# Scores of the diagonal and of neighbours by element products, the mask added in PSUM, and the last two output tiles finished in SBUF

## The reference

```python
u = rmsnorm(x, g_mix); proj = u @ w_in          # columns: q k v | hg_q hg_f hg_i hg_og | gate_a gate_b
# A: stick-breaking attention, 8 heads of 128, strictly causal
z = q @ k.T * scale
log_keep = where(s < t, log_sigmoid(-z), 0); later = reverse_cumsum(log_keep) - log_keep
w = exp(where(s < t, log_sigmoid(z) + later, -inf)); y_a = w @ v
# B: HGRN2 recurrence, 8 heads, state 128 x 128:  S_t = diag(f_t) S_{t-1} + (1-f_t)^T v_t,  o_t = q_t S_t
y_b = rmsnorm(o) * silu(hg_og)
m = sigmoid(gate_a) * (y_a @ p_a) + sigmoid(gate_b) * (y_b @ p_b)
h = x + m @ w_o
up = causal_depthwise_conv(rmsnorm(h) @ w_up, width 3); gate, val = split(up)
out = h + (silu(gate) * val) @ w_down            # d_ff = 5632
```

## Time and profile before

| | us |
|---|---|
| median of 3 runs | 2868.12 (2868.11 to 2868.18) |
| profiled execution | 2867.83 |
| its span | 2866.3 |
| PE busy | 2844.1 (99%) |
| DVE busy | 1852.0 (65%) |
| ACT busy | 1175.4 (41%) |
| POOL busy | 283.5 (10%) |

### The profile page before, as it was taken

One profiled execution on the slowest core, in us unless ns is written; L12 is line 12 of the kernel. 1 busy time (PEld: TensorE's weight loads), 2 busy tenths in 40 slices (PEclk: granted clock), 3 DMA queues, 4 the chain that ended last, 5 costly groups with the idle time before them and its releaser, 6 DMA issues.

```text
span 2866.3 us, 46361 instructions
## 1 busy us (share of the span) xinstructions
PE 2844.1 (99%) x16324; PEld 2504.7 (87%) x16324; DVE 1852.0 (65%) x3256; ACT 1175.4 (41%) x1575; POOL 283.5 (10%) x384
## 2 busy tenths in 40 slices
PE   8999999999999999999999999999999999999998
PEld 6888888888888888888889999999999999999997
DVE  6545454545454546444458988878878887887883
ACT  5333323232323233333345544444444444454443
POOL 1000101020201000000000111101111111110112
PEclk9999999999999999999999999999999999999999
DMA  4242425252423332444445655556555565555657
GB/s 159 79 138 84 146 84 148 92 149 89 114 93 96 97 92 96 155 146 139 139 160 156 141 137 139 134 137 137 137 137 133 137 140 131 140 135 135 139 136 144
DMA packets 157157, 366.96 MB, mean 128 GB/s; under 512 B 18192, under 2 KB 27536, under 8 KB 156560
## 3 DMA queue, kind: packets, MB, share of 16 engines
q1 hardware_dynamic: 111888, 273.41, 30.4%
q0 software_dynamic: 45056, 90.72, 17.4%
HBM read 303.24 MB, written 78.12 MB: 133 GB/s over the span
## 4 chain that ended last, share of the span: by engine, by line
PE 97%; DMA 1%; issue 1%; DVE 0%; POOL 0%; ACT 0%; SPq 0%; POOLq 0%; ACTq 0%; DVEq 0%
PE bank L1440 15%; PE bank L1442 15%; PE bank L1441 15%; PE bank L1604 10%; PE bank L1606 10%; PE bank L1605 10%; PE bank L1622 5%; PE bank L1621 5%; PE bank L1623 5%; PE bank L1486 2%; PE bank L1473 1%; PE bank L1531 1%; PE bank L1517 1%; DMA w_raw<-wstream 0%; POOL out_t L509 0%
## 5 line engine op out<-in xcount | busy, mean ns | idle before, releaser
L1604 PE MATMUL bank<-v_hi,w_hi 128*128 128x256 f32 x2464 | 698.0, 283 | 2.1 <-issue 1.5
L1606 PE MATMUL bank<-v_hi,w_lo 128*128 128x256 f32 x2464 | 697.3, 283 | 0.0
L1605 PE MATMUL bank<-v_lo,w_hi 128*128 128x256 f32 x2464 | 697.3, 283 | 0.0
L720 ACT ACTIVATE w_hi<-w_raw 128x896 fp32r<-128x896 f32 (+1 forms) x528 | 444.8, 846 | 555.2 <-DVE w_raw L1245 390.7
L1440 PE MATMUL bank<-u_hi,w_hi 128*128 128x512 f32 x1408 | 555.2, 394 | 11.0 <-DVE u_lo L894 10.3
L1252 DVE TENSOR_TENSOR w_lo<-w_raw,w_hi 128x896 fp32r<-128x896 f32 (+1 forms) x528 | 499.5, 952 | 102.1 <-ACT w_hi L720 101.0
L1442 PE MATMUL bank<-u_hi,w_lo 128*128 128x512 f32 x1408 | 549.5, 390 | 0.0
L1441 PE MATMUL bank<-u_lo,w_hi 128*128 128x512 f32 x1408 | 549.0, 390 | 0.0
L868 DVE TENSOR_TENSOR w_lo<-w_raw,w_hi 128x1024 fp32r<-128x1024 f32 x240 | 292.7, 1222 | 341.0 <-ACT w_hi L527 338.8
L1604 PEld LDWEIGHTS bank<-v_hi,w_hi 128*128 128x128 f32 x2464 | 472.8, 192 | 5.5 <-issue 3.8
L1605 PEld LDWEIGHTS bank<-v_lo,w_hi 128*128 128x128 f32 x2464 | 472.9, 192 | 1.8 <-issue 0.2
(11 more groups left out here) (210 smaller groups left out, 3303.8 us busy)
## 6 DMA issues: line engine op xcount, KB each, us to landing
w_raw<-wslots SPq DMA_DIRECT2D x504, 256.0 KB, 2.7
w_raw<-wstream SPq DMA_DIRECT2D x240, 512.0 KB, 3.5
out_t<-stage POOLq DMA_DIRECT2D x168, 256.0 KB, 4.3
sums_scratch<-wfirst POOLq DMA_DIRECT2D x24, 448.0 KB, 11.6
w_raw<-sums_scratch SPq DMA_DIRECT2D x24, 448.0 KB, 3.3
gates_scratch<-g_out POOLq DMA_DIRECT2D x32, 256.0 KB, 2.6
g_in<-gates_scratch POOLq DMA_DIRECT2D x16, 512.0 KB, 4.0
x_in<-x_t SPq DMA_DIRECT2D x8, 512.0 KB, 9.9
```

The source lines that it names most:

```text
L720: act.activation(w4_hi[ring][:, 0:width], w4_raw[ring][:, 0:width], ACT.Copy).then_inc(w4_hi_ready, 1)
L1604: nc.tensor.matmul(out, wh, xh, start=kp == 0 and half == 0, stop=False, skip_group_check=True)
L1605: nc.tensor.matmul(out, wh, xl_, start=False, stop=False, skip_group_check=True)
L1606: ins = nc.tensor.matmul(out, wl, xh, start=False, stop=kp == KP - 1, skip_group_check=True)
```

## The change

1. The mask matmuls are gone. PE's z_done comes after the four score matmuls, DVE adds the mask (now fp32 in SBUF) to the four diagonal blocks in PSUM, and ACT waits for z_masked.
2. The diagonal scores and the level-0 scores (each token with its left neighbour in a pair) are sums over channels of element products. DVE multiplies them into prod (512 + 256 columns), ACT copies prod to prod_hi (fp32r), DVE subtracts to prod_lo, and PE sums over partitions with a matmul of ones against prod_hi and prod_lo. Level 0 is left out of `levels`, and DVE's copy of k into xl at level 0 is gone.
3. The last two down tiles are not copied by ACT and not added by POOL. SP loads the present sums of output tiles 14 and 15 into SBUF, DVE adds the PSUM banks, and SP stores plainly. Tile 15 is computed in two halves of 256 columns in banks 0 and 1 (in_halves: for each half, three matmuls of 256 columns per f, and half_done after the first half of the last slot).

```diff
@@ SP, after the weight loads
+            sp_.wait_ge(slot_done, SLOTS - RING)
+            sp_.dma_start(part_sum[:, :], out_t[:, c * SEQ:]).then_inc(part_sum_in, 16)
+            sp_.wait_ge(last_ready, 1)
+            sp_.dma_start(out_t[:, c * SEQ:(c + 1) * SEQ], last_out[:, 0:SEQ]).then_inc(last_stored, 16)
+            for half in range(2):
+                at_ = SEQ + HALF * half
+                sp_.wait_ge(last_ready, 2 + half)
+                sp_.dma_start(out_t[:, c * SEQ + at_:c * SEQ + at_ + HALF],
+                              last_out[:, at_:at_ + HALF]).then_inc(last_stored, 16)
+            sp_.wait_ge(last_stored, 16 * 3)
@@ POOL
-            for d, c in DOWNS:
+            for d, c in DOWNS[:-LAST]:
@@ ACT
-                            act.wait_ge(z_done, per(1, 1))
+                            act.wait_ge(z_masked, per(1, 1))
...
                             act.wait_ge(vt_done, per(2, 2))
                             act.activation(v_tok[:, :], misc_b[:, :], ACT.Copy).then_inc(vt_ready, 1)
+                            act.wait_ge(prod_ready, per(2, 2))
+                            act.activation(prod_hi[:, :], prod[:, :], ACT.Copy).then_inc(prod_hi_ready, 1)
@@ DVE, level(0)
-                    steps.did(dve.tensor_copy(X[:, :, 0, :], K[:, :, 0, :]))
...
+                if L == 0:
+                    pairs = prod[:, SEQ:NP].rearrange("p (g r) -> p g r", r=1)
+                    dve.tensor_tensor(pairs, X[:, :, 1, :], K[:, :, 0, :], ALU.mult).then_inc(prod_ready, 1)
@@ DVE, p == 6 + 3 * late
+                            dve.wait_ge(z_done, per(1, 1))
+                            for b in range(NB):
+                                ins = dve.tensor_tensor(Z[b][:, b * P:(b + 1) * P], Z[b][:, b * P:(b + 1) * P],
+                                                        mask[:, :], ALU.add)
+                            ins.then_inc(z_masked, 1)
@@ DVE, p == 11 + late and p == 12 + late
                             take(5, v_in[:, :])
+                            dve.tensor_tensor(prod[:, 0:SEQ], qn[:, :], kn[:, :], ALU.mult).then_inc(prod_ready, 1)
                             level(0)
                             level(1)
...
+                            dve.wait_ge(prod_hi_ready, per(1, 1))
+                            dve.tensor_tensor(prod_lo[:, :], prod[:, :], prod_hi[:, :].bitcast(F32),
+                                              ALU.subtract).then_inc(prod_lo_ready, 1)
                             level(2)
                             level(3)
@@ DVE, at the end
+            dve.wait_ge(part_sum_in, 16)
+            dve.wait_ge(slot_done, SLOTS - 1)
+            dve.tensor_tensor(last_out[:, 0:SEQ], bank[GROUP + DOWNS[-2][0] % GROUP][:, :], part_sum[:, 0:SEQ],
+                              ALU.add).then_inc(last_ready, 1)
+            for half in range(2):
+                at_ = HALF * half
+                if half == 0:
+                    dve.wait_ge(half_done, 1)
+                else:
+                    dve.wait_ge(slot_done, SLOTS)
+                dve.tensor_tensor(last_out[:, SEQ + at_:SEQ + at_ + HALF],
+                                  bank[half][:, 0:HALF],
+                                  part_sum[:, SEQ + at_:SEQ + at_ + HALF], ALU.add).then_inc(last_ready, 1)
@@ PE, after unit 6
-                                nc.tensor.matmul(Z[b][:, b * P:SEQ], kn[:, b * P:(b + 1) * P], qn[:, b * P:SEQ],
-                                                 start=True, stop=False, skip_group_check=True)
-                                ins = nc.tensor.matmul(Z[b][:, b * P:(b + 1) * P], ident_r[:, :], nmask_r[:, :],
-                                                       start=False, stop=True, skip_group_check=True)
+                                ins = nc.tensor.matmul(Z[b][:, b * P:SEQ], kn[:, b * P:(b + 1) * P], qn[:, b * P:SEQ],
+                                                       start=True, stop=True, skip_group_check=True)
@@ PE, after unit 13
-                            for b in range(NB):
-                                nc.tensor.matmul(Z[2][:, b * P:(b + 1) * P], kn[:, b * P:(b + 1) * P],
-                                                 qn[:, b * P:(b + 1) * P], start=True, stop=True)
+                            pe.wait_ge(prod_lo_ready, per(1, 1))
+                            for part in (prod_hi, prod_lo):
+                                nc.tensor.matmul(Z[2][:, :], ones_r[:, :], part[:, 0:SEQ],
+                                                 start=part is prod_hi, stop=part is prod_lo)
+                            for part in (prod_hi, prod_lo):
+                                nc.tensor.matmul(Z[0][:, 0:NP - SEQ], ones_r[:, :], part[:, SEQ:NP],
+                                                 start=part is prod_hi, stop=part is prod_lo)
@@ PE, last tile
+                    if d == DOWNS[-1][0]:
+                        ins = in_halves(ring, kk, fs, first)
+                        continue
```

More of the change, by code:

```diff
@@ L65 @@
 STAGES, END_STAGES, END = 2, 8, 168
+LAST = 2
 def feed_forward_slots():
@@ L126 @@
 EXP_LN_SET, SIGMOID_SET = 6, 2
-DVE_STEPS1, ACT_STEPS1 = 110, 18
+DVE_STEPS1, ACT_STEPS1 = 108, 18
 class Steps:
@@ L179, in build_program @@
     at = R3 + 12 * NZ
+    NP = SEQ + SEQ // 2
+    prod, prod_lo = sb("prod", NP, 32 * 1024), sb("prod_lo", NP, 32 * 1024, F32R)
+    prod_hi = sb("prod_hi", NP, 32 * 1024 + 4 * NP, F32R)
     S = sb("S", NB * SEQ, at)
@@ L202, in build_program @@
     ident_r = sb("ident_r", P, c0 + 12 * P, F32R)
-    nmask_r = sb("nmask_r", P, c0 + 16 * P, F32R)
+    mask = sb("mask", P, c0 + 16 * P)
     ones_r = sb("ones_r", P, c0 + 20 * P, F32R)
@@ L231, in build_program @@
     stage_end = [sb(f"stage_end{j}", SEQ, R2 + T * j) for j in range(END_STAGES)]
+    part_sum = sb("part_sum", LAST * SEQ, R2 + T * END_STAGES)
+    last_out = sb("last_out", LAST * SEQ, R2 + T * (END_STAGES + LAST))
     u_sum, v_sum, g_sum = sb("u_sum", HALF, 28 * K), sb("v_sum", HALF, 29 * K), sb("g_sum", SEQ, 30 * K)
@@ L271, in build_program @@
     qk_ready, vt_done, vt_ready = sem("qk_ready"), sem("vt_done"), sem("vt_ready")
-    z_done, log1p_ready, sp_ready = sem("z_done"), sem("log1p_ready"), sem("sp_ready")
+    z_done, z_masked, log1p_ready, sp_ready = sem("z_done"), sem("z_masked"), sem("log1p_ready"), sem("sp_ready")
     sp_hi_ready, sp_lo_ready, c_done, prob_ready = (
@@ L278, in build_program @@
     yb_ready = sem("yb_ready")
+    prod_ready, prod_hi_ready, prod_lo_ready = sem("prod_ready"), sem("prod_hi_ready"), sem("prod_lo_ready")
     sums_step = [sem(f"sums_step{j}") for j in range(4)]
@@ L301, in build_program @@
     stage_free = sem("stage_free")
+    part_sum_in, half_done, last_ready, last_stored = (
+        sem("part_sum_in"), sem("half_done"), sem("last_ready"), sem("last_stored"))
     act_step, dve_step = sem("act_step"), sem("dve_step")
@@ L409, in _ @@
                     load_slot(r * RING + ring, ring)
+            _, c = DOWNS[-LAST]
+            d = max(d for d, c_ in DOWNS[:-LAST] if c_ >= c)
+            for e in range(d + 1 - STAGES, d + 1):
+                _, done, value = stage_of(e)
+                sp_.wait_ge(done, value)
+            sp_.wait_ge(slot_done, SLOTS - RING)
[8 more added lines that the diff above has]
+            sp_.wait_ge(last_stored, 16 * 3)
         @block.gpsimd
@@ L514, in _ @@
                     seen += 1
-            for d in range(seen, len(DOWNS)):
+            for d in range(seen, len(DOWNS) - LAST):
                 _, done, value = stage_of(d)
@@ L848, in position @@
                         for c, d, _, _, last in TABLE[n - 1][1]:
-                            if last:
+                            if last and d < len(DOWNS) - LAST:
                                 take_down(n, d, slots_done)
@@ L858, in _ @@
                 position(n)
-            take_down(SLOTS, len(DOWNS) - 1, SLOTS)
         @block.vector
@@ L904, in _ @@
             dve.tensor_copy(ones_r[:, :], ones[:, :])
-            steps.did(dve.tensor_copy(nmask_r[:, :], nmask[:, :]))
+            steps.did(dve.tensor_copy(mask[:, :], nmask[:, :]))
             dve.wait_ge(x_sq_ready, 2)
@@ L972, in level @@
                 steps.did(dve.tensor_tensor(X[:, :, 1, :], Q[:, :, 1, :], F_[:, :, 1, :], ALU.mult))
-                steps.wait(1)
+                steps.wait(L > 0)
+                if L == 0:
+                    pairs = prod[:, SEQ:NP].rearrange("p (g r) -> p g r", r=1)
+                    dve.tensor_tensor(pairs, X[:, :, 1, :], K[:, :, 0, :], ALU.mult).then_inc(prod_ready, 1)
                 steps.did(dve.tensor_tensor(F_[:, :, 1, :], F_[:, :, 1, :],
@@ L1069, in phase1_body @@
                                 take(2, v_in[:, :])
+                        if p == 6 + 3 * late:
+                            dve.wait_ge(z_done, per(1, 1))
[3 more added lines that the diff above has]
+                            ins.then_inc(z_masked, 1)
                         if p == 7 + 3 * late:
@@ L1607, in up_slot, with in_halves @@
```

(13 more changed lines are left out.)

## The result

The changed kernel takes **2850.45 us** (median of 4 runs, 2849.7 to 2851.03) against 2868.15 us for the kernel before on the same chip (4 runs, 2868.11 to 2868.55): ratio 0.9938 with a 95% interval of 0.9921 to 0.9955, 17.7 us less. I had forecast 12.2 us less, 2855.9 us, with a range down to 2852.8. The direction was right and the gain too small by 5.5 us; the time lies 2.3 us under the range.

What follows compares the result with a forecast made beforehand. The prediction took PE as the bound, its chain covering 97% of the span. Terms 3.6 + 8.6 - 1.8 + 1.8 = 12.2 us less gave 2855.6 us profiled, 2855.9 us as median, range 2852.8 to 2860.2.

Steps and rivals of the forecast that it cites:

- Part 1: Mask in phase 1: score block 2.39 us instead of 2.84 in each of eight heads, 3.6 us less.
- the cover in front of the cumulative matmuls: Before L1531's matmuls: sp_lo ends 3.3 us before PE uses it, so DVE's mask adds cost 0.
- Part 2: Diagonal and neighbour scores in phase 1: block 3.62 us instead of 4.70, 8.6 us less, against 1.8 us of new stalls.
- link by link sum: Chain before head 2's scores: prod_hi 0.85, prod_lo 0.95, levels 2.90 us, ending 239.7; PE loads at 239.53, short about 0.15.
- Rivals A: New chain before the scores is longer, PE stalls 0.5 to 1.5 us every head: 2862.1 us at 1 us; chance 0.12.
- D: DVE's wait for prod_hi loses over 1.75 us a head, slower than before: 2874.1 us at 2.5; chance 0.03.
- Part 3: End of the kernel: last store lands at 2860.3 instead of 2862.1, 1.8 us sooner.
- Rival B: New chain in phase 1 just fits without stalls and the end gives 2.8 us: 2853.1 us; chance 0.13.

Runs made afterwards that it cites:

- parts 1 and 2 alone: Kernel before with DVE's mask add and the diagonal and neighbour scores by products, the end left as before: 2856.91 us, ratio 0.9963.
- e_late: Changed kernel with ACT's prod_hi one position later, behind the next weight split: 2857.56 us, ratio 0.9964.
- e_pool_wait: Changed kernel where SP still issues the last three stores but POOL, not SP, waits for their landing: 2853.85 us, ratio 0.9952.
- e_pool_store: Changed kernel with the last three plain stores issued and waited for by POOL in place of SP: 2855.03 us, ratio 0.9956.
- e_pool_pe2: Changed kernel where POOL, its own stores landed, waits at the end for PE's last slot; SP as before: 2851.99 us, ratio 0.9945.
- e_act_wait2: Changed kernel where ACT, not SP, waits for the landing of the last three stores: 2850.2 us, ratio 0.9937.
- e_sp_waits: Kernel before where SP, not POOL, waits for the last eight accumulating stores, which POOL still issues: 2866.2 us, ratio 0.9995.

## Why the prediction fell short

**Part 1, right.** The forecast was 2.39 us for the block and 3.6 us in all; the block measures 2.39, and the mask alone brought 3.5. The add in PSUM, for which no row stood, took 0.292 us, only slightly more than its neighbour's 0.278, and the cover in front of the cumulative matmuls held it. Groups by form on DVE and ACT in the changed kernel, then the timeline of head 2 at the place of the earlier trace rows:

```profile
L1099 DVE TENSOR_TENSOR bank<-bank,mask 128x128 f32<-128x128 f32 x32 | 7.1, 292 | 20.7 <-PE bank L1569 20.7
...
L1136 DVE TENSOR_TENSOR prod_lo<-prod,prod_hi 128x768 fp32r<-128x768 f32 x8 | 7.7, 958 | 12.7 <-ACT prod_hi L673 12.7
```
```profile
L673 ACT ACTIVATE prod_hi<-prod 128x768 fp32r<-128x768 f32 x8 | 6.7, 838 | 0.0
```
```profile
207.61 1.48 DVE L1113 TENSOR_TENSOR sp_lo<-sp,sp_hi 128x1280 fp32r<-128x1280 f32 x1
...
211.47 0.39 PE L1581 MATMUL bank<-sp_hi,ntri_r 128*128 128x512 f32 x1
```

sp_lo ends at 209.09, 2.4 us ahead of its use. It was 3.3 in the earlier trace rows, and the 0.9 that went are the adds, as forecast.

**Part 2, right in mechanism, 0.7 us too dear.** The forecast had a block of 3.62 us and stalls of 0.15 us in seven heads and 0.75 in the first, 1.8 together. In the profile the block runs from 238.67 to 242.34, 3.67 us, a pause of 0.07 included; the stalls are 7 x 0.07 + 0.58 = 1.1 us. By these terms phase 1 should have gained 3.6 + 8 x 1.1 - 1.1 = 11.3 us; the marks show 10.5 in the changed kernel and 11.4, counted from the first matmul, in the one with parts 1 and 2 alone, which is the scatter of a single profile. The link by link sum was good: prod_hi 0.84 (forecast 0.85), prod_lo 0.96 (0.95), and PE waiting on just this chain. Rivals A (0.5 to 1.5 us a head) and D fall; e_late shows that A was only one misplaced ACT instruction away.

**Part 3, the step that failed:** "and the span ends 4.2 us later". I took the 4.2 us between the last landing and the end of the span as a constant of every program, held it fixed ("and 4.2 to the end of the span"), and so compared landings only; my own remark that the end might gain 2.8 us "with a shorter wind-up once POOL is done early" gave it and a faster store a microsecond together. It was POOL's own way out, its DRAIN of 3.7 us with 0.5 around it, which begins at POOL's last wait. In the changed kernel POOL's last store is issued here,

```profile
2838.67 0.85 POOL L533 DMA_DIRECT2D out_t<-stage_end  x1 [1.87 <-ACT stage_end L805]
```

so that, with 4.2 us to land and some 3.8 to the end of its DRAIN, it is done at 2846.6, under the work of the others and 1.9 us ahead of SP, which leaves last, in 0.4. That is 4.2 - 0.4 = 3.8 us. The second size in this step was SP's store: 1.7 us instead of 2.3, 0.6 us more. By the Trainium skill (DMA: Bandwidth & Descriptors, Anatomy of one DMA) a 128 KB transfer would take an estimated 2.3 us and a 256 KB one 2.6. That section gives its fit for DMAs that GpSimd issues, and I had used it for a store by SP. SP's stores here took 1.7 and 2.0, POOL's of the same sizes (the kernel with POOL's plain stores) 2.0 to 2.1 and 2.3, and the measurement decides.

**The rest.** 3.8 + 0.6 = 4.4 of the 5.4 us between the forecast for the profiled run (2855.6) and its time (2850.21). The remaining 1.0 is 0.8 in phase 4 (0.2 forecast as a cost, 0.6 measured as a gain) and 0.2 elsewhere. PE's pauses in phase 4 that are put down to issue are 0.6 us in all here and 1.5 in the kernel before, and 0.4 to 2.0 over all fourteen profiles, whose phase 4 lasts 1370.4 to 1371.4 us. I count this as scatter and not as an effect of the change, the 0.8 included.

Rival B came nearest (end gives more), with the right place and less than half of the size.

## What to carry to other kernels

The time from the last landing to the end of the span is not a constant: look which engine holds the last wait, and let the one that leaves slowest (here POOL) have its last instruction and its last wait early, with another engine waiting for the final stores. The rows of the DRAINs show which engine that is; they stand under the line that opens the block of all engines (L368 before, L377 after). Moving the wait alone was not enough while POOL had a store of its own in flight. Where a chain has no slack left, price each link by a row of the same shape, and check the order of instructions on each engine in it: one ACT copy in the wrong place cost 7 us of the 17.7.

## What the runs showed of the hardware

- POOL needs 4.0 to 4.2 us from its last wait to the end of the span, for a DMA's landing (e_pool_wait 4.0, e_pool_store 4.2, kernel before 4.2) as for a matmul (e_pool_pe2 4.06). Of that its DRAIN is 3.54 (e_pool_wait, e_pool_pe2) to 3.78 us (e_pool_store). SP and ACT need 0.4 (changed kernel, e_act_wait2), with DRAINs of 7 and 8 ns. With an accumulating store of its own in flight and no wait for it (e_sp_waits), POOL's DRAIN took 7.2 us and the span ended 6.7 us after the issue had; this stays unexplained.
- With little else in flight, at the end of the kernel, a plain 128 KB store to DRAM lands in 1.7 to 1.8 us from SP and in 2.0 to 2.1 from POOL, a plain 256 KB one in 2.0 from SP and in 2.3 from POOL (e_pool_store), and the last 256 KB accumulating store in 4.0 (kernel before) to 4.3 (e_sp_waits). The accumulating stores before it, among other transfers, took up to 9.8 us (changed kernel).
- A 128x128 DVE add in PSUM, read and written there, takes 292 ns, against 278 for the one that reads PSUM and writes SBUF.
- Over the fourteen profiles, each of another kernel with the same start, PE's first matmul came between 8.8 and 10.6 us. How much of this is scatter of one and the same kernel isn't shown.
